# First norm turned by a diagonal of reciprocal roots, with products of two slabs between its tiles and decay/beta on four strips

## What is computed

```python
h = _rms_norm(x, norm_mix_pre)          # x * rsqrt(mean(x^2) + eps) * gain
p = h @ w_in                            # 1024 -> 5640 columns
qa, ka, va, qkv_b, z_b, a_b, b_b, gate_a, gate_b = jnp.split(p, split_at, axis=-1)
...
g = -jnp.exp(a_log) * jax.nn.softplus(a_b + dt_bias)    # decay, 4 heads
beta = jax.nn.sigmoid(b_b)                              # 4 heads
```

## Time and profile before

| | |
|---|---|
| median of 3 runs | 2053.22 us |
| profiled execution | 2055.41 us, its span 2053.7 us |
| PE / DVE / ACT / POOL busy | 95% / 36% / 31% / 29% |
| mean granted clock of TensorE | 0.979 |

### The profile page before, as it was taken

The page is one execution under the profiler, slowest core; times in us unless marked ns, Lnnn a source line. Parts: engine busy times, 40 slices in busy tenths (PEclk is TensorE's granted clock), DMA queues, the critical chain, the costliest instruction groups (busy, mean ns, idle before and its releaser), DMA issues. The chain is left out here.

```text
span 2053.7 us, 34074 instructions
## 1 busy us (share of the span) xinstructions
PE 1951.6 (95%) x13954; PEld 1763.4 (86%) x13954; DVE 743.2 (36%) x1467; ACT 633.8 (31%) x1239; POOL 602.7 (29%) x466
## 2 busy tenths in 40 slices
PE   5999999999998888899799999999999999999998
PEld 4999999999995566688699879999999999999996
DVE  4111577211116654555564173222222222222225
ACT  5100232110005664344363245222222222222222
POOL 6111111122113001644254244333333333333333
PEclk7999999999999998999999999999999999999999
DMA  5122222622217323031054232111111111111123
GB/s 138 56 92 91 75 87 87 236 94 92 88 56 251 103 83 83 3 107 58 22 177 131 103 113 86 48 41 41 43 49 43 42 41 42 41 42 41 43 76 149
DMA packets 159271, 169.18 MB, mean 82 GB/s; under 512 B 14187, under 2 KB 130043, under 8 KB 159150
## 3 DMA queue, kind: packets, MB, share of 16 engines
q1 hardware_dynamic: 152814, 141.52, 22.6%
q10 hardware_dynamic: 6336, 25.96, 3.2%
HBM read 126.84 MB, written 40.55 MB: 82 GB/s over the span
## 5 line engine op out<-in xcount | busy, mean ns | idle before, releaser
L2282 DVE TENSOR_TENSOR t_acc<-t_acc,t_B 128x512 f32<-128x512 f32 x252 | 173.1, 687 | 541.0 <-PE t_B L2375 541.0
L116 PE MATMUL i_ps<-x_hi,i_w_lo 128*128 128x384 f32 x1056 | 353.9, 335 | 0.0
L116 PE MATMUL i_ps<-x_hi,i_w_hi 128*128 128x384 f32 x1056 | 353.7, 335 | 0.0
L116 PE MATMUL i_ps<-x_lo,i_w_hi 128*128 128x384 f32 x1056 | 353.7, 335 | 0.0
L2362 PE MATMUL t_B<-t_merged_hi,t_wm_lo 128*128 128x384 f32 x768 | 257.0, 335 | 1.0 <-POOL t_wm_lo L1987 1.0
L2362 PE MATMUL t_B<-t_merged_lo,t_wm_hi 128*128 128x384 f32 x768 | 256.6, 334 | 0.0
L2362 PE MATMUL t_B<-t_merged_hi,t_wm_hi 128*128 128x384 f32 x768 | 256.6, 334 | 0.0
L106 POOL TENSOR_TENSOR i_w_lo<-i_w_raw,i_w_hi 128x1024 fp32r<-128x1024 f32 x44 | 104.9, 2386 | 444.1 <-ACT i_w_hi L101 444.1
L1987 POOL TENSOR_TENSOR t_wm_lo<-t_raw,t_wm_hi 128x1024 fp32r<-128x1024 f32 x49 | 118.9, 2426 | 295.7 <-ACT t_wm_hi L2062 295.7
L116 PEld LDWEIGHTS i_ps<-x_hi,i_w_lo 128*128 128x128 f32 x1056 | 199.0, 188 | 0.0
L116 PEld LDWEIGHTS i_ps<-x_lo,i_w_hi 128*128 128x128 f32 x1056 | 198.9, 188 | 0.0
(11 more groups left out here) (324 smaller groups left out, 3405.7 us busy)
## 6 DMA issues: line engine op xcount, KB each, us to landing
proj<-i_out ACTq DMA_DIRECT2D x44, 576.0 KB, 2.8
i_w_raw<-in_w_in SPq DMA_DIRECT2D x44, 512.0 KB, 3.9
t_raw<-in_w_up SPq DMA_DIRECT2D x32, 512.0 KB, 4.4
t_raw<-in_w_down SPq DMA_DIRECT2D x32, 512.0 KB, 3.6
t_gates<-proj SPq DMA_DIRECT2D x48, 192.0 KB, 2.6
a_k_cache<-in_cache_attn_k SPq DMA_DIRECT2D x8, 1024.0 KB, 5.4
a_v_cache<-in_cache_attn_v SPq DMA_DIRECT2D x8, 1024.0 KB, 5.4
d_c<-proj SPq DMA_DIRECT2D x3, 1536.0 KB, 7.1
```

The source lines that it names most:

```text
L116: last = pe.matmul(out, a[s][:, c, :], b[:, c, tokens], start=k == 0, stop=k == n - 1)
L2282: dve.tensor_tensor(a, a, B[(ND * j + d) % 4][:, :], ALU.add).then_inc(added, 1)
```

## The change

- **Diagonal.** DVE no longer scales the tile. It multiplies the 128×128 identity by the reciprocal roots (`diag`, two buffers), and PE turns the raw tile by a plain F32 matmul with that diagonal (L304 of the changed code) in the place of the transpose.
- **Low parts shared.** POOL makes the low part of the even halves, DVE that of the odd ones (two semaphores); `h` has six buffers, not four; ACT's high parts follow two tiles behind, not three.
- **Slabs 0 and 1 in the norm.** They are loaded behind tiles 4 and 5, split by ACT after its turns for tiles 5 and 6 and by POOL between its low parts. Their products of the first token group stand, in halves of 12 matmuls, behind tiles 5 to 8 on PE, the second group's after them, the third's after the state rows. The six PSUM banks of the projection are allocated before the norm for this, and the norm's ring uses two of them. The loop over slabs starts with slab 2; DVE's copies and ACT's stores of slabs 0 and 1 stand ahead of it.
- **Decay and beta on strips.** Their weights are no longer split: 8 columns are padded with zeros to 32, and 48 plain F32 matmuls put four partial sums on four strips of 32 output rows. DVE copies all 128 rows, and the small matmuls that turn them add the strips up (`strips`, four identities below each other).

The core of the diff:

```diff
+    RING, HRING = 4, 6
...
+        own = [c.enter_context(nc.psum_tensor(f"n_ps{i}", [P, 512], F32)) for i in range(2)]
+        banks = [own[0], own[1], env.ps[NTG - 1], env.ps[2 * NTG - 1]]
+        ps = [bank[:, :].rearrange("p (k t) -> p k t", t=P) for bank in banks]
+        r = NB * (CW - 1)
+        pst = own[0][:, 0:CC * r].rearrange("p (k r) -> p k r", r=r)
...
-        AHEAD = 3
+        AHEAD = 2
+        SLAB_AT = (4, 5)
...
                 sp.dma_start(x[:, t, :], xp[t] if t < NPT else xs).then_inc(xl[t], 16)
-
-            sp.dma_start(env.wab[:, :, :], w_in[:, :, COL_AB:COL_GATE]).then_inc(env.ab_land, 16)
-            for s in range(WRING):
-                sp.dma_start(w.raw[s][:, :, :], w_in[:, :, s * P:(s + 1) * P]).then_inc(w.landed[s], 16)
+                if t in SLAB_AT:
+                    n = SLAB_AT.index(t)
+                    sp.dma_start(w.raw[n][:, :, :], w_in[:, :, n * P:(n + 1) * P]).then_inc(w.landed[n], 16)
+
+            sp.wait_ge(wab_clear, 1)
+            sp.dma_start(env.wab[:, :, 0:2 * HB], w_in[:, :, COL_AB:COL_GATE]).then_inc(env.ab_land, 16)
...
                 if t >= AHEAD:
                     for g in range(2 * (t - AHEAD), 2 * (t - AHEAD) + 2):
                         split(act, g)
+                if t - 1 in SLAB_AT:
+                    split_hi(act, w, 0, SLAB_AT.index(t - 1))
...
-                dve.tensor_scalar(x[:, t, :], x[:, t, :], rstd[:, t:t + 1], None, ALU.mult).then_inc(scaled, 1)
+                if t == 0:
+                    dve.wait_ge(const, 3)
+                dve.tensor_scalar(diag[:, t % 2, :], env.ident[:, :], rstd[:, t:t + 1], None, ALU.mult
+                                  ).then_inc(diag_made, 1)
...
+                if t >= 3:
+                    split_low(dve, 2 * t - 5)
...
-            for g in range(2 * NT):
-                split_low(pool, g)
+            pool.sem_inc(w.lo_made, WRING)
+            for t in range(NT):
+                split_low(pool, 2 * t)
+                if t + 1 in SLAB_AT:
+                    split_lo(pool, w, 0, SLAB_AT.index(t + 1))
...
+            pe.sem_inc(w.prod, env.credit)
+
+            def products(sl, g, part):
+
+                tokens = slice(g * TG, (g + 1) * TG)
+                if part == 0:
+                    pe.wait_ge(w.lo_made, sl + 1 + WRING)
+                    pe.wait_ge(lo_even, NTG * (g + 1))
+                    pe.wait_ge(lo_odd, NTG * (g + 1))
+                for cc in range(part * DC // 2, (part + 1) * DC // 2):
+                    for a, b in ((w.lo, env.x_hi), (w.hi, env.x_lo), (w.hi, env.x_hi)):
+                        last = pe.matmul(env.ps[NTG * sl + g][:, 0:TG], a[sl][:, cc, :], b[:, cc, tokens],
+                                         start=cc == 0 and a is w.lo, stop=cc == DC - 1 and a is w.hi and b is env.x_hi)
+                if part == 1:
+                    last.then_inc(w.prod, 1)
...
+            for t in range(NT):
+                pe.wait_ge(diag_made, t + 1)
+                for g in (2 * t, 2 * t + 1):
+                    if g >= RING:
+                        pe.wait_ge(gained, g - RING + 1)
+                    for k in range(4):
+                        cc = 4 * (g % 2) + k
+                        last = pe.matmul(ps[g % RING][:, k, :], x[:, t, cc * P:(cc + 1) * P], diag[:, t % 2, :],
+                                         start=True, stop=True)
+                    last.then_inc(turned, 1)
+                if t >= NT - 4:
+                    products((t - NT + 4) // 2, 0, t % 2 ^ (NT - 4) % 2)
+            for sl in range(2):
+                for part in range(2):
+                    products(sl, 1, part)
+            pe.wait_ge(gained, 2 * NT)
...
+            for sl in range(2):
+                for part in range(2):
+                    products(sl, 2, part)
...
+        rows = (row_bank, pab_bank, row_bank)
...
-            act.wait_ge(ab_land, 16)
-            act.activation(wab_hi[:, :, :], wab[:, :, :], ACT.Copy).then_inc(ab_hi, 1)
             for s in range(2):
-                split_hi(act, w, 0, s)
+                split_hi(act, w, 1, s)
+                act.wait_ge(free, 3 * s + 3 + CREDIT)
+                act.dma_start(env.proj[s * P:(s + 1) * P, :], st[s][:, :]).then_inc(sent[s], 16)
...
-            dve.wait_ge(ab_rows, 1)
+            dve.tensor_reduce(strips[:, :], env.ident[:, :].rearrange("p (j c) -> p c j", j=4)[:, 0:2 * HB, :], AX.X, ALU.add
+                              ).then_inc(ab_read, 1)
+            for s in range(2):
+                for g in range(NTG):
+                    dve.wait_ge(prod, 3 * s + g + 1 + CREDIT)
+                    dve.tensor_copy(st[s][:, g * TG:(g + 1) * TG], ps[3 * s + g][:, 0:TG]).then_inc(free, 1)
             for g in range(NTG):
-                dve.tensor_copy(ab_row[:, g * TG:(g + 1) * TG], ps[g][0:2 * HB, 0:TG]).then_inc(ab_read, 1)
+                dve.wait_ge(ab_rows, g + 1)
+                dve.tensor_copy(ab_row[:, g * TG:(g + 1) * TG], rows[g][:, 0:TG]).then_inc(ab_read, 1)
...
+            pe.wait_ge(ab_land, 16)
             for g in range(NTG):
-                k = 0
-                for cc in range(DC):
-                    for a, b in ((wab_hi, env.x_lo), (wab_lo, env.x_hi), (wab_hi, env.x_hi)):
-                        last = pe.matmul(ps[g][0:2 * HB, 0:TG], a[:, cc, :], b[:, cc, g * TG:(g + 1) * TG],
-                                         start=k == 0, stop=k == 3 * DC - 1)
-                        k += 1
-            last.then_inc(ab_rows, 1)
-            pe.wait_ge(ab_read, NTG)
+                if g == 2:
+                    pe.wait_ge(ab_read, 2)
+                for k in range(2 * DC):
+                    part = (env.x_lo, env.x_hi)[k // DC]
+                    last = pe.matmul(rows[g][32 * (k % 4):32 * (k % 4) + 32, 0:TG], wab[:, k % DC, :],
+                                     part[:, k % DC, g * TG:(g + 1) * TG].bitcast(F32), start=k < 4, stop=k >= 2 * DC - 4)
+                last.then_inc(ab_rows, 1)
+            pe.wait_ge(ab_read, NTG + 1)
             for n in range(2 * NT):
                 first = TP + 64 * n if n < 2 else 64 * (n - 2)
                 for x in range(2):
                     last = pe.matmul(pab[64 * x:64 * x + 64, n, :], ab_row[:, first:first + 64],
-                                     env.ident[0:2 * HB, 0:2 * HB], start=True, stop=True)
+                                     strips[:, :], start=True, stop=True)
             last.then_inc(ab_made, 1)
-            with pe.Fori(0, HALF) as i:
+            with pe.Fori(1, HALF) as i:
```

More of the change, by code:

```diff
@@ L139, in stage_norm_in @@
         rstd = c.enter_context(nc.sbuf_tensor("n_rstd", [P, NT], F32))
-        h = c.enter_context(nc.sbuf_tensor("n_h", [P, RING, 4, P], F32))
+        h = c.enter_context(nc.sbuf_tensor("n_h", [P, HRING, 4, P], F32))
+        diag = c.enter_context(nc.sbuf_tensor("n_diag", [P, 2, P], F32))
         st = c.enter_context(nc.sbuf_tensor("n_state", [NB * (CW - 1), CONV], F32))
-        ps = [c.enter_context(nc.psum_tensor(f"n_ps{i}", [P, 4, P], F32)) for i in range(RING)]
-        pst = c.enter_context(nc.psum_tensor("n_pst", [P, CC, NB * (CW - 1)], F32))
+        own = [c.enter_context(nc.psum_tensor(f"n_ps{i}", [P, 512], F32)) for i in range(2)]
[3 more added lines that the diff above has]
+        pst = own[0][:, 0:CC * r].rearrange("p (k r) -> p k r", r=r)
         xp = I["x_prompt"].rearrange("a (t p) d -> (a t) p d", p=P)
@@ L156, in split, with split_low @@
             act.wait_ge(gained, g + 1)
-            act.activation(out_of(env.x_hi, g), h[:, g % RING, :, :], ACT.Copy).then_inc(hi_made, 1)
+            act.activation(out_of(env.x_hi, g), h[:, g % HRING, :, :], ACT.Copy).then_inc(hi_made, 1)
         def gain(dve, g):
             dve.wait_ge(turned, g + 1)
-            if g >= RING:
-                dve.wait_ge(hi_made, g - RING + 1)
-                dve.wait_ge(lo_made, g - RING + 1)
+            if g >= HRING:
+                dve.wait_ge(hi_made, g - HRING + 1)
+                dve.wait_ge(lo_odd if g % 2 else lo_even, (g - HRING) // 2 + 1)
             half = g % 2
-            dve.tensor_tensor(h[:, g % RING, :, :], ps[g % RING][:, :, :],
+            dve.tensor_tensor(h[:, g % HRING, :, :], ps[g % RING][:, :, :],
                               bc(env.gains[:, 0, 4 * half:4 * half + 4], 2, P), ALU.mult).then_inc(gained, 1)
[L168 to L171, removed]
+        def split_low(eng, g):
+            eng.wait_ge(hi_made, g + 1)
+            eng.tensor_tensor(out_of(env.x_lo, g), h[:, g % HRING, :, :],
+                              out_of(env.x_hi, g).bitcast(F32), ALU.subtract
+                              ).then_inc(lo_odd if g % 2 else lo_even, 1)
         @block.sync
@@ L229, in _ @@
             gain(dve, 2 * NT - 1)
+            for t in range(NT - 3, NT):
+                split_low(dve, 2 * t + 1)
             dve.wait_ge(st_turned, 1)
@@ L301, in stage_in_proj @@
         y = [staged(f"i_y{i}", [P, T]) for i in range(2)]
```

(19 more changed lines are left out.)

27 lines of the change are left out of this document (6 added, 21 removed).

## The result

The changed kernel takes 2040.36 us in the median of 5 runs (2037.77 to 2045.85), the kernel before 2053.22 beside it: ratio 0.9929, 95% interval 0.9915 to 0.9943. The forecast was 2040.5. The profiled execution was the slowest of the five, 2045.85 us (span 2044.1).

What follows compares the result with a forecast made beforehand. PE bounds the projection; its open time lies in the first 58 us. Start 23.5 + work 43.95 + clock 2.5 put slab 2 at 69.95, its first copy 12.7 us earlier: 2040.5 from the median 2053.22, range 2034 to 2049.

Steps and rivals of the forecast that it cites:

- the marker: Slab 2's first copy out of PSUM, in the input projection: forecast at 76.75 us in place of 89.47, 12.7 earlier.
- Start of the products, 23.5: In the norm: PE begins slab 0's products at 23.5 us, bounds 1 us earlier to 3 later.
- PE from there: PE's work from slab 0's first product to slab 2's start, clock loss aside: seven terms, sum 43.95 us.
- Strips 8.3: Decay and beta stage: 48 F32 matmuls, 96 records of 384 columns on four strips, take 8.3 us.
- Turning 3.0: After the decay products: turning the strips still takes 72 records on PE, 3.0 us.
- Clock 2.5: Before slab 2: half-clock loss on PE, at the first products and after the turning, adds 2.5 us (0 to 5).
- Cover of 4.6 us for slab 2's load: Slab 2 is loaded and split by 65.4 us, 4.6 before PE wants it at 70.
- Rival A: Decay products: the strips do not overlap, 33.6 us in place of 8.3, 2065.8 in all, slower; chance 0.06.
- Rival B: Norm tiles: a matmul with the diagonal streams four times, 3.74 us a tile, 2054.0 in all, no change; chance 0.04.
- Rival C: Norm: DVE and POOL hold each other up, products start 5.1 us later, 2046.2 to near 2049 in all; chance 0.14.
- Rival D: Norm to slab 2: PE's clock does not fall at all, 2038.0 to 2035.5 us in all; chance 0.10.
- The gain from the median: Whole kernel: what slab 2 gains the end gains, taken off the median 2053.22 us, giving 2040.5.

Runs made afterwards that it cites:

- (1): The changed kernel itself, unchanged, run again beside other experiments: median 2040.0 us, ratio to the kernel before 0.9923.

## Why the prediction was right

The mechanism was right: PE's open time was filled, the strips overlap, and the marker came 13.9 us earlier for a forecast of 12.7. That the marker is off by no more than 1.2 (75.57 for 76.75) is partly errors of opposite sign, and that the time is off by 0.14 us is luck, since runs of one kernel lie 8 us apart.

- *Start of the products, 23.5:* 25.07, and 27 in other executions, inside the bounds (22.5 to 26.5) only in some. The step that failed is the square of tile 3 at 12.3: it came at 14.16, since tile 0 on PE took 3.54 where a tile takes 1.95, and ACT's splits of tile 0 waited for the gains behind it. Then ACT's 2.41 a tile held exactly in this execution; in four of seven DVE set 3.30.

```profile
13.62 0.63 ACT L163 ACTIVATE x_hi<-n_h 128x512 fp32r<-128x512 f32 x1 [0.83 <-DVE n_h L171]
14.16 1.04 ACT L214 ACTIVATE n_junk<-n_x 128x1024 f32<-128x1024 f32 x1
```

- *PE from there:* the two slabs, the tiles and the state take 33.3 (25.07 to 58.4), by terms 31.5 and 1.7 for a clock spell. A tile is 1.95 with its tail, foreseen 1.87 (the next product starts 1.71 behind its start); 2.59 in the spell; the state 0.92 (0.9); the stage's end 0.32 (0.4).
- *Strips 8.3:* 7.94 (58.70 to 66.64). *Wait 0.75:* 0.67. *Turning 3.0:* 2.27. The row of before was taken at a mean clock of 0.70 (its window, 54.7 to 57.8 us), which the term overlooked; here the clock is 1.00.
- *Clock 2.5:* two spells of 3.4 us, one in the products, one at slab 2, each costing 1.7 (0.81 of 9 us and 0.76 of 7 us make both lengths); the second was priced at 5.1 us long by slab 0's of before. In all 2.0 too much from the products to slab 2's start and 0.75 behind it, against 1.6 too little at the start.
- *Cover of 4.6 us for slab 2's load:* 1.2. Its low half was ready near 68.3, half of POOL's 4.69 behind 65.94, and PE began at 69.52. The load landed 5.8 us after its issue, not 3.9. It held, barely.
- *Rival A:* false as the code stands. By the spacing within one strip, serial strips would cost 0.32 a record, near the 0.35 it was priced at; order alone made 9.2 of its 25.3 us happen. The Trainium skill ("TensorE: Matmul & The Clock Gate", Measured speedup vs the span model) gives 3.07 for four row tiles; these column strips reach 0.32/0.081, nearly 4, and the measurement decides.
- *Rival B:* false, 1.95 a tile and not 3.74.
- *Rival C:* there in the small, in some executions, at 2 us and not at 5, and before the products only: between 24 and 35 us diagonals of 1.0 to 1.4 and subtractions of 1.8 are covered by PE's twelve products a tile. It came in four of seven executions, and was given 0.14.
- *Rival D:* in the profiled execution true in the norm (clock 1.00 from 16 to 25 us), false right behind it; in run (1) true up to 76 us. The reading that with transposes alone the clock stayed at 0.50 holds from 18.4 us on the earlier trace rows; from 15 to 18.4 it was 1.00 there.
- *The gain from the median:* 12.9 there, 13.9 at the marker, 9.6 between the two profiled spans. That the end gains what slab 2 gains did not hold in this pair: 4.1 us went to the clock behind 971 us. It is right only within the 8 us by which executions differ.

## What to carry to other kernels

Where an engine is full behind a slow prologue, later work that is moved into the prologue's gaps is gained as far as it really fills them (here some 5 of 8.3 us), and work moved within the full stretch (the turning) gains nothing but its waits. Small matmuls on strips paid nearly fourfold here when the code went round the strips matmul by matmul, and twofold when four in a row stayed on one strip. And take a marker inside the trace for parts that are smaller than what executions of one kernel differ by.

## What was not expected of the hardware

- DVE and POOL, both on SBUF alone, hold each other up as if only one could work: in (1) DVE's diagonal, begun at 16.30, ends at 17.68, when POOL's subtraction (16.34 to 17.61) is done. Some tenths of a us decide whom it costs: 0.29 to 1.38 for DVE's diagonal, or 1.27 to 1.66 for POOL's subtraction. DVE reading PSUM beside POOL (diagonal 0.35, two gains 1.28) was not stretched. A diagonal that starts at 15.86 or at 16.30 so makes 2.41 or 3.30 us a tile for the tiles behind it.
- PE's first tile takes 3.5 to 3.8 us in each execution with the diagonal, as at half clock. A view from 9.0 to 12.5 reads 1.00 only because no clock is recorded there. What decides whether the first record begins near 12.4 or near 14.4 us stays open; the rhythm followed it in all seven executions.
- The starts of 27 are given back: (1) begins 2.1 later than the first trace and has its marker 0.4 earlier (slab 4's first copy 1.1 earlier; slab 2's waits for DVE's gates in (1)), since neither spell of half clock occurs in it (granted clock 1.00 in every stretch from 16 to 76 us).
